# A decoder block with product-key experts: the gates made by one-hot products on TensorE instead of a grid in DRAM, and an unsplit UP product over 144 tokens

## What is computed

```python
v1, i1 = lax.top_k(s1, PEER_TOPK)          # 16 of 128, for each of 8 heads
v2, i2 = lax.top_k(s2, PEER_TOPK)
...
top, pos = lax.top_k(cand, PEER_TOPK)      # 16 of 16 x 16 sums
idx = jnp.take_along_axis(cand_idx, pos, axis=-1)   # i1 * 128 + i2
g = jax.nn.softmax(top.astype(jnp.float32), axis=-1)
u = u_tab[idx]
vv = v_tab[idx]
act = jax.nn.gelu(jnp.einsum('thkd,td->thk', u, hb)) * g
return jnp.einsum('thk,thkd->td', act, vv)
```

## Time and profile before

| | us |
|---|---|
| median of 3 runs | 1761.17 |
| lowest and highest run | 1757.84, 1763.6 |
| the profiled execution (its span) | 1758.1 |
| in it: all before UP's first matmul | 551.1 |
| UP, first matmul to the end of the last | 608.6 |
| gap to DOWN's first matmul | 3.2 |
| DOWN, 2560 matmuls | 580.5 |
| what follows DOWN's last matmul | 14.7 |

### The profile page before, as it was taken

One profiled execution on the slowest core, in us unless ns is written; L12 is line 12 of the kernel. 1 busy time (PEld: TensorE's weight loads), 2 busy tenths in 40 slices (PEclk: granted clock), 3 DMA queues, 4 the chain that ended last, 5 costly groups with the idle time before them and its releaser, 6 DMA issues.

```text
span 1758.1 us, 28277 instructions
## 1 busy us (share of the span) xinstructions
PE 1732.3 (99%) x9480; PEld 1517.9 (86%) x9480; DVE 1535.3 (87%) x2469; ACT 799.5 (45%) x1185; POOL 603.1 (34%) x413
## 2 busy tenths in 40 slices
PE   7999999999999999999999999999999999999998
PEld 5888888644999999999999999988888888888886
DVE  4668899967688898998999999989999999999997
ACT  3001222300545555556555555554455544555454
POOL 1000000011000388788688888613321211112110
PEclk9999999999999999999999999999999999999999
DMA  9999986699798777987899999999999999999994
GB/s 380 421 421 422 424 322 252 234 387 417 301 349 272 219 218 223 296 253 224 249 382 389 399 411 404 401 365 411 414 413 410 390 404 398 397 399 389 407 387 190
DMA packets 142648, 617.22 MB, mean 351 GB/s; under 512 B 45347, under 2 KB 45939, under 8 KB 87411
## 3 DMA queue, kind: packets, MB, share of 16 engines
q1 hardware_dynamic: 80530, 410.04, 60.0%
q0 software_dynamic: 55712, 202.52, 31.9%
q10 hardware_dynamic: 6336, 3.75, 0.7%
HBM read 598.19 MB, written 16.89 MB: 350 GB/s over the span
## 4 chain that ended last, share of the span: by engine, by line
PE 76%; DMA 9%; DVE 8%; POOL 4%; issue 2%; ACT 1%; DVEq 0%; ACTq 0%; POOLq 0%; SPq 0%
PE ps L1448 33%; PE ps L1110 14%; PE ps L1117 9%; DMA raw<-in_w_ada 7%; PE ps L1161 5%; PE ps L1331 5%; POOL weights L570 3%; PE ps L1172 2%; DVE raw L1547 2%; PE ps L1103 2%; PE ps L1277 2%; DMA early<-in_w_front 1%; DVE w_low L1489 1%; DVE big L1603 1%; POOL big L555 1%
## 5 line engine op out<-in xcount | busy, mean ns | idle before, releaser
L805 ACT ACTIVATE w_hi<-raw 128x1024 fp32r<-128x1024 f32 x444 | 468.8, 1059 | 458.6 <-PE ps L1448 187.4
L1489 DVE TENSOR_TENSOR w_low<-raw,w_hi 128x1024 fp32r<-128x1024 f32 x444 | 541.5, 1224 | 85.5 <-ACT w_hi L805 77.6
L570 POOL DMA_INDIRECT weights<-sel x192 | 366.0, 1906 | 69.2 <-issue 57.6
L1110 PE MATMUL ps<-a,w_hi 128*128 128x384 f32 x1920 | 383.9, 341 | 0.8 <-issue 0.8
L1110 PEld LDWEIGHTS ps<-a,w_hi 128*128 128x128 f32 x1920 | 326.9, 189 | 1.6 <-issue 1.0
L1448 PE MATMUL ps<-w_low,a 128*128 128x512 f32 x1024 | 273.8, 389 | 0.0
L1448 PE MATMUL ps<-w_hi,a 128*128 128x512 f32 x1056 | 268.1, 389 | 1.5 <-ACT big L918 1.5
L1117 PEld LDWEIGHTS ps<-a,w_low 128*128 128x128 f32 x1920 | 247.1, 191 | 2.6 <-DVE w_low L1489 2.3
L1117 PE MATMUL ps<-a,w_low 128*128 128x192 f32 x1920 | 248.2, 271 | 0.7 <-DVE w_low L1489 0.6
L1448 PEld LDWEIGHTS ps<-w_hi,a 128*128 128x128 f32 x1056 | 198.2, 188 | 42.6 <-ACT big L918 1.6
L1448 PEld LDWEIGHTS ps<-w_low,a 128*128 128x128 f32 x1024 | 192.3, 188 | 39.8
(11 more groups left out here) (240 smaller groups left out, 2008.2 us busy)
## 6 DMA issues: line engine op xcount, KB each, us to landing
raw<-in_peer_u SPq DMA_DIRECT2D x128, 1024.0 KB
raw<-in_peer_v SPq DMA_DIRECT2D x256, 512.0 KB
early<-in_w_front SPq DMA_DIRECT2D x56, 1024.0 KB, 11.4
raw<-in_w_ada POOLq DMA_DIRECT2D x48, 1024.0 KB, 9.6
raw<-in_w_ada SPq DMA_DIRECT2D x32, 1024.0 KB
raw<-in_peer_wq SPq DMA_DIRECT2D x16, 1024.0 KB
big<-in_w_gate_f POOLq DMA_DIRECT2D x16, 1024.0 KB, 6.0
weights<-third SPq DMA_DIRECT2D x16, 768.0 KB, 19.1
```

What stands on the lines that cost most here:

```text
L570: gp.indirect_dma_start(weight_elements, bass.IndirectOffsetOnAxis(ap=put_at[:, c:c + 1], axis=0), put_gate[:, c:c + 1], None, compute_op= ...
L805: act.activation(high_at(ph, j), raw[:, s % RING, :], ACT.Copy).then_inc(hi_ready, 1)
L1110: done = pe.matmul(ps[:, b % 2, 0:2 * TD].rearrange("p (m t) -> p m t", m=2), high_at(ph, j)[:, k * P:(k + 1) * P], a_pair[:, kc, :, 0:TD] ...
L1489: dve.tensor_tensor(w_low[:, s % RING, :], raw[:, s % RING, :], high_at(ph, j).bitcast(F32), ALU.subtract).then_inc(lo_ready, 1)
```

## The change

- UP multiplies TU = 144 tokens, with all 256 halves plain (`WHOLE`): 16 matmuls of 144 columns a block, from `h_up`, a packed copy of the tokens. No `hi`, `lo`, line 1084 or line 1499 is left in UP. Four PSUM banks in turn take the blocks in place of two.
- TM = 48 tokens (144 to 191) take gathered `u` rows: 64 gathers on 96 partitions ("mid" rows, 0.79 MB each). DVE makes their dot products against `h_mid`, ACT their gelu, and they are put into DOWN's strips. With the last 64 tokens' rows ("end") there are U_ROWS = 64 + 36 = 100 gathers in UP, one `take_rows` each, three buffers. 28 late rows (before 14) stay for DOWN, two in each step of its loop.
- The grid in DRAM, its clearing, the 192 puts and the 32 groups of DOWN are gone. Instead, for every four tokens DVE makes one-hots (`hots`: one instruction of 128x512 and four of 128x128), and PE multiplies them, token by token, into a 128 x 128 grid of gates (`grid`: four matmuls of 128 columns). It does so behind blocks 48 to 83 for the 144 tokens, and behind blocks 97 to 108 for the 48.
- Strips of the first GRID_AT = 48 blocks are gated by DVE straight from PSUM (`gate_made_acts`); ACT copies the other 80 columns of each grid into the strips (`put_grid`), and the blocks from 48 on are gated in groups of four (`gate_ring`).
- The routing (`route`) stands in a row on DVE with nothing between but rows. PE turns the picks in `turn_picks`, behind block 30 for the second token tile and behind block 46 for the first; the latter waits for `picks_made` 2, that is for all 16 routings.

```diff
-PH_UP = Phase(PH_WQ, EXPERT_BLOCKS // 32, 16, plain=(7, 15), groups=tuple(range(22, 30)))
+PH_UP = Phase(PH_WQ, EXPERT_BLOCKS // 8, 16, plain=WHOLE)
...
-            def put_weights(n):
...
-                gp.indirect_dma_start(weight_elements, bass.IndirectOffsetOnAxis(ap=put_at[:, c:c + 1], axis=0),
-                                      put_gate[:, c:c + 1], None, compute_op=ALU.add).then_inc(weights_put[tt], 16)
...
+                        done = pe.matmul(ps[:, b % 4, 0:TU], raw[:, s % RING, k * P:(k + 1) * P], h[:, kc, 0:TU],
+                                         start=kc == 0, stop=kc == KC - 1)
...
+            def grid(q):
+
+                pe.wait_ge(hot_made, q + 1)
...
+                for t in range(4):
+                    done = pe.matmul(ps[:, 4 + q % 4, t * KEYS:(t + 1) * KEYS], picks_now[q % 2][:, 0, t, :],
+                                     picks_now[q % 2][:, 1, t, :], start=True, stop=True)
...
+                if n == PICKS_TURNED_AT[1]:
+                    turn_picks(1, 1)
+                if n == PICKS_TURNED_AT[0] - 1:
+                    turn_picks(0, 2)
+                if 0 <= n - GRID_AT < QUADS:
+                    grid(n - GRID_AT)
...
+            for b in range(PEER_HEADS):
+                route(2 * b + 1)
+                if b:
+                    finish_head(b - 1)
+                take_rows(2 if b > 2 else 0)
+            for b in range(PEER_HEADS):
+                route(2 * b)
...
+                take_rows(2)
+            mid_tables()
+            finish_first()
+            hots(0)
+            hots(1)
+            for q in range(QUADS):
+                if q + 2 < QUADS:
+                    hots(q + 2)
+                if q:
+                    gate_made_acts(q - 1)
+                take_rows(1)
+            gate_made_acts(QUADS - 1)
+            take_rows(ROWS - rows_done[0])
+            ring = 0
+            for n in range(GRID_AT + QUADS + 2, EXPERT_BLOCKS + 1):
+                while GRID_AT + 4 * ring + 4 <= n and not (n < MID_GELU_AT and ring >= 9):
+                    gate_ring(ring)
+                    ring += 1
...
+                if n < EXPERT_BLOCKS:
+                    take_rows(1)
...
-                    if j % 8 == 3 and not (last and j > 8):
-                        make_group(g, i, at(i, 16, 16 * (g // 2 + 1)))
...
-                    if j == LATE_AT and i is not None and not last:
-                        late_dot(i)
+                    if j in LATE_AT and i is not None and not last:
+                        late_dot(LATE_AT.index(j), i)
```

More of the change, by code:

```diff
@@ L75 @@
 PH_WQ = Phase(PH_Q0, BLOCKS // 4 - 1, 8)
-PH_UP = Phase(PH_WQ, EXPERT_BLOCKS // 32, 16, plain=(7, 15), groups=tuple(range(22, 30)))
[L77 to L82, removed]
+WHOLE = tuple(range(16))
+PH_UP = Phase(PH_WQ, EXPERT_BLOCKS // 8, 16, plain=WHOLE)
+PH_DOWN = Phase(PH_UP, EXPERT_BLOCKS // 8, 16)
 N_A, N_W = 5 * KC, 2 * KC + 6 * PAIRS
@@ L102 @@
 ROWS = PEER_HEADS * TOPK // SLICES
[L103 to L116, removed]
-HEAD_ROWS = ROWS // PEER_HEADS
[L118 to L122, removed]
+LATE_STEPS, LATE_PER, LATE_AT = PH_DOWN.n - 2, 2, (4, 9)
+LATE_ROWS = LATE_STEPS * LATE_PER
+EARLY_ROWS = ROWS - LATE_ROWS
+HEAD_ROWS = ROWS // PEER_HEADS
+ROW_ORDER = [("mid", n) for n in range(ROWS)] + [("end", n) for n in range(EARLY_ROWS)]
+U_ROWS = len(ROW_ORDER)
+ROW_BUFS = 3
+THIRD = 2
+QUADS, MID_QUADS, THIRDS = TU // 4, TM // 4, TU // TM
+GRID_AT = 48
+WINDOW, RING_UP = 40, 8
+MID_GELU_AT, MID_GRID_AT = 90, 97
+PICKS_TURNED_AT = (GRID_AT - 1, 30)
+assert GRID_AT % 4 == 0 and GRID_AT + QUADS < MID_GRID_AT and MID_GRID_AT + MID_QUADS < EXPERT_BLOCKS - 4
+H_UP_FROM = 8
+EXP_AT = (4, 6, 8, 10, 13, 16, 19, 22)
+PACK_AT = (6, 8, 11, 14, 17, 20, 23, 25)
 V_PER = ROWS // PH_DOWN.n
@@ L895, in _ @@
                     copy_scores(u - 2 * KC + 4)
-            for j in range(2):
-                hi(PH_UP, j, None)
             act.wait_ge(split_used, 2 * KC)
@@ L1080, in _, with product @@
         def _(pe):
[L1081 to L1093 removed]
+            def product(n, h):
+                b = B_UP + n
+                if n < 2:
+                    pe.wait_ge(gemm_evac, 10 + 2 * n)
+                elif n < 4:
+                    pe.wait_ge(sc_copied, 8)
+                else:
+                    pe.wait_ge(gemm_evac, b - 3)
+                pe.wait_ge(landed[b % 4], 16 * (b // 4 + 1))
@@ L1094, in product @@
                 for half in range(2):
-                    if half and (b > B_UP or i is not None) and not by_vector(ph, n - 1, i):
-                        add_low(b - 1, i, ph.blocks)
-                    if ahead:
-                        ahead(2 * n + half, i)
-                    s, j = ph.s + 2 * n + half, 2 * n + half
-                    if j in ph.plain:
-                        for k in range(UCH):
-                            kc = half * UCH + k
-                            done = pe.matmul(ps[:, b % 2, 0:TD], raw[:, s % RING, k * P:(k + 1) * P],
-                                             h_full[:, kc, 0:TD], start=False, stop=False, skip_group_check=True)
-                        done.then_inc(split_used, 1)
-                        continue
```

775 lines of the change are left out of this document (360 added, 415 removed).

## The result

The changed kernel takes 1876.62 us (median of 4 runs, 1875.74 to 1881.12) against 1760.38 us for the kernel before (1757.84 to 1763.6): a ratio of 1.0659, with a 95% interval of 1.064 to 1.0677. It is slower by 116 us. The forecast of 1761 us and its range up to 1784 were wrong, and so was every rival: the slowest of them stood at 1802.

What follows compares the result with a forecast made beforehand. TensorE was taken to bound UP and DOWN. Terms: 26 + 3 (first wait) + 14 (DMA late in UP) - 44 (TensorE's work) - 0.4 + 1 = -0.4 us, so a median of 1761 us, range 1742 to 1784.

Steps and rivals of the forecast that it cites:

- TensorE's own work in UP: UP: 3.98 us a block, 565 us in all against 608.6 before, so TensorE alone would gain 44 us.
- price of a mid row: UP, blocks with grids: block and 0.79 MB row need 376 GB/s in 4.88 us, under 413, so nothing is late.
- first stretch: UP to the second turn of the picks: VectorE sets the end, TensorE idles 26 us, plus 3 for slow restart.
- second stretch: UP, 36 blocks with grids: TensorE sets the pace, 4.88 us each, 175.5 us, to 959.5.
- Third stretch: UP, blocks 84 to 127: DMA sets it, 200 us, 14 beyond TensorE's pace, bounds 186 and 214.
- step into DOWN: From UP's end to DOWN's first matmul: some 2.8 us, against 3.2 before.
- rival 3: DOWN: two late rows a step hold up `v` rows in POOL's queue, 1768 to 1775 us; chance 0.07.
- +1: DOWN: added time taken as 1 us, bounds 0 and +14, VectorE's and DMA's extra work being covered by TensorE.
- Rival 4: UP: lower memory ceiling of 358 GB/s, or a lower clock, +41 us, 1802 us; chance 0.04.
- Rival 2: UP: the gather's round trip over three buffers paces VectorE, whose late rows delay TensorE, 1780 us; chance 0.14.

Runs made afterwards that it cites:

- kernel with wide rows: The changed kernel with each of the 64 gathers of mid rows on all 128 partitions in place of 96: 1793.39 us, ratio 1.0188.
- packed kernel: The changed kernel with the 48 middle tokens' picks packed on all 128 partitions, 48 gathers in place of 64: 1781.03 us, ratio 1.0119.

## Why the prediction was wrong, point by point

**TensorE's own work in UP: right.** A block was to take 3.98 us. Here nothing waits (a float32 matmul leaves two records, as in the earlier trace rows, so 128 are four blocks):

```profile
572.39 15.85 PE L1026 MATMUL ps<-big,raw 128*128 128x144 f32 x128
588.07 12.17 PE L1026 MATMUL ps<-early,raw 128*128 128x144 f32 x98
```

Four blocks took 588.07 - 572.39 = 15.68 us, 3.92 each.

**The step that failed: the price of a mid row.** "The DMA needs 1.05 MB for the block and 0.79 MB for the row in 4.88 us, 376 GB/s, under the 413 of DOWN. Nothing of this is late by itself". I priced the row by its bytes, with a ceiling read from gathers that all had 128 partitions. No row of the trace of before has a large transfer on fewer, and I did not bound that case, though the change makes 64 of them. The first stretch had no term for its bytes at all. At 59.0 us of engine time for a MB of rows and 57.3 for one of blocks, 0.79 and 1.05 MB take (46.6 + 60.1) / 16 = 6.7 us. The pace measured was 6.25 us, since in these 219 us only 34 blocks and 33 rows had to be fetched (35.87 and 25.95 MB); the others lay in the ring and the row buffers already. The error stands in both of the first stretches. With 128 partitions, and a third more bytes, the second stretch keeps a grid each 4.83 us (783.22 to 952.11 in 35 steps), as predicted (4.88).

**First stretch: right where the cause above is taken away.** The picks were to be ready at 776, with a wait of 26 us. The kernel with wide rows has its turned picks at 772.96 behind 17.31 us of idleness, and at 770.76 behind 20.56 us with ScalarE's waits away: the time was right to 6 us, the wait at the lower end of its bounds (18 and 38) or just under it. In the changed kernel the wait is not seen: slow weights hold TensorE back until the routing is done. What was missing is ScalarE. I costed the packs at nothing, without looking at what their waits in `pack_head` queue up behind them. They cost nothing here, where DMA is full, and in the packed kernel, where it is not, 16 us together with the routing's wait.

**Third stretch: the mechanism right, the size small.** DMA sets it, at 405 to 421 GB/s. With the step into DOWN it took 213 us where the prediction has 203 (its bounds, 186 and 214, are without that step of 2.8). In the kernel with wide rows it is 219 us, above the bound of 214 and the step. There TensorE also waits once for the one-hots of the mid rows, which the sum did not have:

```profile
1033.24 2.07 PE L1073 MATMUL ps<-early 128*128 128x128 f32 x8 [11.47 <-DVE early L1845]
```

**DOWN: near rival 3 in size, not in mechanism.** It pays 17 us, where +1 was taken and up to 14 allowed. Rival 3 had POOL's order and late `v` rows in mind. But in DOWN VectorE never waits for a row, and what comes late is blocks. 8 blocks, 4 `v` rows and 2 late rows are 14.7 MB in a step of 36.3 us, 405 GB/s, and with 14 late rows fewer, or with late rows of 16 partitions, DOWN is back at 580.4 and 581.0 us. I had taken the mean over DOWN (396 GB/s) against the best 100 us (413) and called the difference room. The column beside it said otherwise: at 392 GB/s the share was 0.99, at 413 it was 1.02. The DMA engines were already full. Full engines alone are no loss, since TensorE did not pause in DOWN before. Why the same 228 MB take longer with more of them in gathers stays open.

**The rivals.** Rival 4 came nearest, "a lower ceiling", and was given 0.04. It looked for the limit in the memory, and the row of blocks alone at 420 GB/s spoke against that rightly. What makes the ceiling is the shape of the transfers that share the engines. Rival 2, the gather's round trip, did not decide. In the second stretch of the changed kernel VectorE waited 9 us for rows and 55 us for TensorE's grids.

The Trainium skill (DMA: Bandwidth & Descriptors, The descriptor swizzle) says that in a transfer of 128 partitions each engine writes through one port of SBUF, its own. The runs agree with what would follow from it: any shape dealt out otherwise has engines writing through each other's ports, and then its own packets and those of the weights take longer. But no run here shows which engine writes which partition, so this mechanism is argued, and only the price by shape is shown. The Trainium skill (SBUF — State Buffer, Door 1: The DMA port swizzle) makes bandwidth depend on how many of the 16 ports the partitions reach. Partitions 0 to 95 reach all 16 on its table, and so do 0 to 111; by this rule alone they should do as well as 128, and the runs disagree, with 286 and 284 GB/s against 420.

## What to carry to other kernels

A large gather that shares the DMA engines with other transfers should be on 128 partitions, in one piece, even if a part of it is thrown away. (Only gathers of 8 KB rows were tried here.) Price a transfer by the share of the engines that it takes and not by its bytes, and take room from the share column: GB/s under a ceiling seen elsewhere is no room where the share is 1.0. Where two engines are late for the same point, taking away one wait may show nothing, so try both before calling either of them harmless.

## What the runs showed of the hardware that I had not expected

- Gathers of rows of 8 KB beside weight blocks of 1 MB on 128 partitions moved 420 GB/s with the gathers on 128 partitions, 280 on 96, 284 on 112, 282 on 64, and 237 as two halves of 64, each time at a share of 1.01 or 1.02.
- The slow shape slows its neighbours: the weights' packets, unchanged, cost 57 us of engine time for a MB beside gathers on 96 partitions and 69 us beside two halves of 64, in place of 39.
- The granted clock fell to 0.93 in the changed kernel's UP, where TensorE kept pausing for 2 to 4 us for weights, and was 1.00 in the stretches where it did not.
